# A delta-rule chunk scan: its triangular inverse in compact blocks of 32, and the head norms and turned outputs taken by groups

## The chip, the cores and the metric

The kernel runs on one core of one Trainium2 chip, as one program. The metric is device time in microseconds (us) for one execution, inputs in HBM to output in HBM. The kernel before took a median of 3159.22 us in 3 runs (3155.52 to 3159.49).

## The reference

Two models of two layers each are run one after the other on 256 tokens of width 1024. The change lies in the last mixer of the second model, a delta rule over 512 tokens (256 of context, 256 of the sequence), 16 heads of 64, in both directions, and in what follows it. (One small edit is at the kernel's very start.)

```python
def rwkv7_scan(r, w, k, v, kk, a, S):
    def step(S, inp):
        rt, wt, kt, vt, kkt, at = inp
        sa = jnp.einsum("bhvk,bhk->bhv", S, -kkt)
        S = S * wt[:, :, None, :] + sa[..., None] * (kkt * at)[:, :, None, :] + vt[..., None] * kt[:, :, None, :]
        return S, jnp.einsum("bhvk,bhk->bhv", S, rt)

def rwkv_out(y, p, kvec, lnx, w_o):
    y = head_layernorm(from_heads(y), lnx[0], lnx[1], RW_HEADS, r.dtype)   # mean and variance over each head's 64
    bonus = jnp.sum((r * k * kvec[2]).reshape(bn, L, RW_HEADS, RW_HEAD), axis=-1, keepdims=True) * v...
    return ((y + bonus.reshape(bn, L, D)) * g) @ w_o
```

## The kernel before

The kernel is written by hand, engine by engine: each engine has one program, and semaphores (`signal(...)`) join them. Each instruction of VectorE, ScalarE and GpSimd waits for the one before it on its engine (`Line.turn`, L72); TensorE's wait only where the code says so. Most of the kernel is matrix products in three passes (`x_high`, `x_low`, `w_high`, `ring_low`); these are not touched.

**The scan** is done in chunks of 64 tokens: 8 chunks forward, then 8 in the other direction, so 16 steps n, and one round more (n = 16) that finishes the last. The 16 heads stand as two groups g of 8; a group's 8 heads stand as four columns a by two halves i of the 128 partitions. Inside a chunk the delta rule is a lower triangular system, and the kernel inverts its matrix by products. The helper `quarters` does for each (a, i) one 64x64 by 64x64 product in fp32: eight products an operation (`one`), sixteen for two (`pair`). Each product in fp32 stands in the trace as two LDWEIGHTS and two MATMUL. The product for i = 0 uses rows and columns 0 to 63 of the array, that for i = 1 rows and columns 64 to 127.

One chunk of one group takes twelve steps, S0 to S11, and each `yield` in `scan_pe`, `scan_act`, `scan_dve` and `scan_pool` ends one:

- S0: `cum` (sums of the log decays) of chunk n and `w` of chunk n-1. S1: `us` of n-1. S2: `lta` of n (the two attention matrices), then `y` of n-1 (only where the chunk belongs to the sequence: n-1 = 4 to 7 and 12 to 15, called late) and `s` (the state) of n-1.
- S3: `n2`. S4: `n3`, `n4`. S5: `p`. S6: `f0`, `m2`. These invert the blocks of 8 on the diagonal.
- S7 to S11: `q2`, `m3`, `q3`, `m4`, `q4` join blocks of 8 to 16, 16 to 32 and 32 to 64; `mt`, `fab` and (late) `rab` lie between, as other operands of the chunk.

Between two steps the result goes from PSUM to SBUF through ScalarE (`n2`, `n4`, `f0`, `m2`, `m3`, `m4`, ...) or VectorE (`tft`, `n3`, `p`, `q2`, `q3`, `q4`, ...). GpSimd masks `lt` for `m2`, `m3`, `m4` (`mj1` to `mj3`). `lead` runs group 0 six steps ahead and then takes the groups in turn, a step of one, a step of the other, on every engine. So S6 of one group stands beside S0 of the other.

**After the scan** (`rwkv_pe`, `rwkv_act`, `rwkv_dve`): VectorE takes the layer norm of all heads in eight instructions over 2048 columns. Then for k = 0 to 7 TensorE turns the rows (`trs`), VectorE copies the halves out, scales, adds and gates them (five instructions a k), and only after k = 7 does TensorE start the output projection with the weights `rwo`, 32 products of 128x128 by 512 columns in fp32. The tiles `rwo` (0,1), (1,0), (1,1) are loaded once the norm's `on_ok` is given, since the scan uses ring slots as scratch.

**At the start** all engines wait for the constants and for the parameters `prm` before their first instruction, VectorE also for x.

Of the kernel before, what the change touches and what calls it, by code (L numbers as in the profile page):

```python
# [16 lines left out]
WS = 2048  # L17
# [173 lines left out]
def tile_plan(dr):  # L191
# [54 lines left out]
    plan.append((("rw2", 1), dr["rw2"], WS))  # L246
    plan.append((("rg2",), dr["rg2"], 1024))
    for n in range(2):
        for g in range(2):
            plan.append((("rwo", n, g), dr["rwo"][n, g], WS))  # L250
# [26 lines left out]
def program(nc, dr, out):  # L277
    ctx = ExitStack()
    with ctx:
# [224 lines left out]
        def norm_act(A, q):  # L504
# [7 lines left out]
            if q == FFN1[0]:  # L512
                split_act(A, ("gu", 0, 0))
            to = XT if q in RAW else xh(cols)
# [36 lines left out]
        def norm_dve(D, q):  # L551
# [3 lines left out]
            if q == FFN1[0]:  # L555
                split_dve(D, ("gu", 0, 0))
            for k in range(8):
# [1771 lines left out]
        joins = C("joins").rearrange("p (z m j) -> p z m j", z=2, m=3)  # L2329
        eye = C("eye")  # L2330
        hs = C("hs")
        PAIR = eye.unsqueeze(1).unsqueeze(1).to_broadcast([128, 2, 4, 64])
# [17 lines left out]
        STFT, SIT, SUT, SATB, SRAB, SKA, SRH = [[blocks(2) for _ in TWO] for _ in range(7)]  # L2350
        SE13 = [unit(2).rearrange("p (k t) -> p k t", k=4) for _ in TWO]
        SAL, SBE, SE2, SLT, SMJ, STD, SMT, SWW, SUS = [[blocks() for _ in TWO] for _ in range(9)]
# [43 lines left out]
        def act_names(n):  # L2396
            new, m = n < 16, n - 1
            return ([(n, "e13"), (n, "e2")] * new + [(m, "w"), (m, "us")] * (n > 0)
                    + [(n, x) for x in ("lta", "n2", "n4", "f0", "m2", "m3")] * new
                    + [(n, "fab")] * (new and feeds(n)) + [(n, "m4")] * new)  # L2400

        def dve_names(n):
            new, m = n < 16, n - 1
            return ([(n, "ak"), (n, "pc"), (n, "tft"), (n, "it")] * new + [(m, "y")] * (n > 0 and late(m))
                    + [(m, "s")] * (n > 0 and feeds(m)) + [(n, x) for x in ("n3", "p", "q2", "mt", "q3")] * new
                    + [(n, "rab")] * (new and late(n)) + [(n, "q4")] * new)
# [3 lines left out]
        def scan_keys(names):  # L2410
# [5 lines left out]
        sc_p = [signal(f"sc_p{g}", [(n, x) for n in range(16) for x in ("br", "mj1", "mj2", "mj3")]) for g in TWO]  # L2416
        on_ok, onr_ok, onn_ok = [signal(n, [0]) for n in ("on_ok", "onr_ok", "onn_ok")]
        yt2_mm, rg_mm, yg_ok = [signal(n, range(8)) for n in ("yt2_mm", "rg_mm", "yg_ok")]
        yc_ok = signal("yc_ok", range(8))
        wo_mm = signal("wo_mm", TWO)  # L2420
# [3 lines left out]
                  "fab": "fab", "m4": "m4"}  # L2424
# [9 lines left out]
        def double(g, key):  # L2434
            return scan_bank(g, key).rearrange("p (y k t) -> p y k t", y=2, k=4)

# [23 lines left out]
        def scan_pe(T, g):  # L2460
            te = T.eng
            al, be, lt, mj, td, mt, ww, us = [x[g] for x in (SAL, SBE, SLT, SMJ, STD, SMT, SWW, SUS)]
# [17 lines left out]
            def one(key, *terms):  # L2480
                take(key)
                quarters(single(g, key), terms, mm(key))

# [5 lines left out]
            for n in ROUNDS:  # L2489
# [25 lines left out]
                if old:  # L2515
                    te.wait_ge(*a_[m, "w"])
                    te.wait_ge(*d_[m, "q4"])
# [13 lines left out]
                yield  # L2531
                if new:
                    te.wait_ge(*d_[n, "tft"])
                    pair((n, "n2"), (tt_, tf), (tf, tt_))
                yield
                if new:
                    te.wait_ge(*d_[n, "it"])
                    te.wait_ge(*a_[n, "n2"])
                    one((n, "n3"), (itt, uu))
                    one((n, "n4"), (uu, tq))  # L2540
                yield
                if new:
                    te.wait_ge(*a_[n, "n4"])
                    te.wait_ge(*d_[n, "n3"])
                    one((n, "p"), (tq, SIT[g][:, 1]))
                yield
                if new:
                    te.wait_ge(*d_[n, "p"])
                    one((n, "f0"), (tf, eye))
                    te.wait_ge(*p_[n, "mj1"])  # L2550
                    one((n, "m2"), (mj, tf))
                yield
                for lev in (2, 3):
                    if new:
                        te.wait_ge(*a_[n, f"m{lev}"])
                        pair((n, f"q{lev}"), (uu, tt_), (tt_, uu))
# [6 lines left out]
                    if new:  # L2563
                        te.wait_ge(*d_[n, f"q{lev}"])
                        te.wait_ge(*p_[n, f"mj{lev}"])
                        one((n, f"m{lev + 1}"), (mj, tf))
                        if lev == 2 and feeds(n):
                            pair((n, "fab"), (al, eye), (be, eye))
                    yield
                if new:  # L2570
                    te.wait_ge(*a_[n, "m4"])
                    one((n, "q4"), (uu, tt_))
                yield

        def scan_act(A, g):
            se = A.eng
            e13, e2, lt, ww, us = [x[g] for x in (SE13, SE2, SLT, SWW, SUS)]
# [10 lines left out]

            for n in ROUNDS:
                new, old, m = n < 16, n > 0, n - 1  # L2590
                if n == 8 and g == 0:
# [15 lines left out]
                if new:  # L2607
                    se.wait_ge(*d_[n, "tft"])
                    if old:
                        se.wait_ge(*p_[m, "mj3"])  # L2610
                    A.copy(lt, double(g, (n, "lta"))[:, 0], a_((n, "lta")))
                yield
                if new:
                    take_both(SUT[g], (n, "n2"))
                yield
                if new:
                    take(tq, (n, "n4"))
                yield
                yield
                if new:  # L2620
                    take(STFT[g][:, 0], (n, "f0"))
                    take(uu, (n, "m2"), -1.0)
                yield
                yield
                if new:
                    take(uu, (n, "m3"), -1.0)
# [4 lines left out]
                if new:  # L2631
                    take(uu, (n, "m4"), -1.0)
                yield
                yield

        def scan_pool(G, g):
# [3 lines left out]
            for n in ROUNDS:  # L2640
# [13 lines left out]
                if new:  # L2654
                    ge.wait_ge(*a_[n, "lta"])
                    G.tt(SMJ[g], SLT[g], bm(joins[:, z, 0, :], 4), ALU.mult, p_((n, "mj1")))
# [4 lines left out]
                if new:  # L2661
                    ge.wait_ge(*mm[n, "m2"])
                    G.tt(SMJ[g], SLT[g], bm(joins[:, z, 1, :], 4), ALU.mult, p_((n, "mj2")))
                yield
                yield
                if new:
                    ge.wait_ge(*mm[n, "m3"])
                    G.tt(SMJ[g], SLT[g], bm(joins[:, z, 2, :], 4), ALU.mult, p_((n, "mj3")))
# [4 lines left out]
        def over(x):  # L2673

            return x.unsqueeze(2).to_broadcast([128, 2, 4, 64])

        def scan_dve(D, g):
# [6 lines left out]
            for n in ROUNDS:  # L2684
# [12 lines left out]
                if new:  # L2697
                    ve.wait_ge(*mm[n, "lta"])
                    D.tt(tft, double(g, (n, "lta")), over(near[:, z:z + 2, :]), ALU.mult, d_((n, "tft")))
# [16 lines left out]
                yield  # L2716
                yield
                if new:
                    ve.wait_ge(*mm[n, "n3"])
                    D.tt(it[:, 1], it[:, 1], single(g, (n, "n3")), ALU.add, d_((n, "n3")))  # L2720
                yield
                if new:
                    ve.wait_ge(*mm[n, "p"])
                    D.tt(tft[:, 1], it[:, 1], single(g, (n, "p")), ALU.add, d_((n, "p")))
                yield
                yield
                for lev in (2, 3):
                    if new:
                        ve.wait_ge(*mm[n, f"q{lev}"])
                        D.tt(tft, tft, double(g, (n, f"q{lev}")), ALU.add, d_((n, f"q{lev}")))  # L2730
# [9 lines left out]
                if new:  # L2740
                    ve.wait_ge(*mm[n, "q4"])
                    D.tt(STD[g], tft[:, 0], single(g, (n, "q4")), ALU.add, d_((n, "q4")))
# [45 lines left out]
        def rwkv_pe(T):  # L2788
# [47 lines left out]
            lead(scan_pe(T, 0), scan_pe(T, 1))  # L2836
            te.wait_ge(*onn_ok[0])
            te.wait_ge(*landed(("rg2",)))
            w = raw(("rg2",))
            for k in range(8):  # L2840
                T.bank(k % 4, yc_ok[k])
                trs(T, [(bank(k % 4)[0:64, 128 * c:128 * c + 128], YZ[:, c, k, :]) for c in FOUR], yt2_mm(k))
                T.bank(4 + k % 4, yg_ok[k])
                T.mm(bank(4 + k % 4)[:, 0:256], w[:, 128 * k:128 * k + 128], GS, True, True,
                     w_free(("rg2",)) if k == 7 else rg_mm(k))
            gate_pe(T, ("r", 0))
            te.wait_ge(*yg_ok[7])
            for n in TWO:
                for g in TWO:
                    key = ("rwo", n, g)  # L2850
                    te.wait_ge(*landed(key))
                    w = raw(key)
                    for tb in TWO:
                        b = 2 * n + tb
                        if g == 0:
                            T.bank(b, wo_d[n] if tb else wo_a[n])
# [536 lines left out]
```

## Time and profile before

| what | us |
|---|---|
| runs, median (lowest to highest) | 3159.22 (3155.52 to 3159.49) |
| profiled execution, its own time | 3160.5 |
| its span in the profile | 3158.7 |
| PE busy / DVE busy / ACT busy / POOL busy | 2906.1 / 1662.3 / 1217.0 / 117.7 |
| granted TensorE clock, mean | 0.953 of full |

PE is TensorE's matmuls, PEld its weight loads, DVE VectorE, ACT ScalarE, POOL GpSimd. All the matmuls of the kernel stand on L165 (a helper), so operations are told apart by tiles and shapes: the scan's are `64*64 64x64`, and run from 2368.7 to 2852.2 us of the span. A matmul's duration (219 ns for 64x64) is its way through the array; many overlap, so the cost of one is the distance between two starts.

### The profile page before, as it was taken

Reading aid. Unit: us, or ns where it says so; the run is one execution under the profiler, and the core shown is the slowest. Engines: PE = TensorE matmul, PEld = TensorE weight load, DVE = VectorE, ACT = ScalarE, POOL = GpSimd, SP = SyncE. Lnnn points to the kernel's source line nnn. Section 1 sums busy time; section 2 is a strip of 40 time slices with the busy share of each in tenths; the row PEclk is TensorE's granted clock in tenths of the full one; section 3 lists DMA queues with packets and bytes.
Section 4 is the critical chain, followed back from the end, with each engine's and each line's share of the span. In section 5 each row is a group of like instructions: output and inputs, shape, how many; then the busy total and the mean of one; then the engine's idle time right before and its main releaser. Section 6 shows DMA issues by size and latency. Waiting matters only on the chain.

```text
span 3158.7 us, 65576 instructions
## 1 busy us (share of the span) xinstructions
PE 2906.1 (92%) x28304; PEld 2435.2 (77%) x28304; DVE 1662.3 (53%) x2467; ACT 1217.0 (39%) x1839; POOL 117.7 (4%) x152
## 2 busy tenths in 40 slices
PE   8999999999999998997977999897999999996997
PEld 8977799898778987776656777673548989993886
DVE  5545655454655554214565777436424544555885
ACT  5445554443555443223433323233113334331333
POOL 0000000000000000000000000000002222220000
PEclk9999999999999999997888999998998999998999
DMA  6444344455443543430001343221200000002343
GB/s 241 180 167 174 122 165 177 174 180 186 165 169 112 184 150 140 173 141 28 2 23 54 147 156 137 100 73 51 94 33 4 4 4 17 4 4 107 133 148 107
DMA packets 49983, 349.87 MB, mean 111 GB/s; under 512 B 5792, under 2 KB 5792, under 8 KB 9248
## 3 DMA queue, kind: packets, MB, share of 16 engines
q1 hardware_dynamic: 49248, 343.56, 30.3%
q8 instruction: 225, 3.69, 0.5%
q0 software_dynamic: 448, 2.11, 0.2%
q14 instruction: 62, 0.51, 0.0%
HBM read 344.61 MB, written 1.05 MB: 109 GB/s over the span
## 4 chain that ended last, share of the span: by engine, by line
PE 78%; DVE 14%; ACT 5%; issue 2%; DMA 1%; DVEq 0%; ACTq 0%; SPq 0%
PE psum L165 78%; DVE arena L98 3%; DVE wide L87 2%; DVE ring_low L87 2%; DVE arena L87 2%; ACT w_high L144 1%; DMA ring<-in_evt 1%; PE psum L170 1%; ACT arena L140 1%; ACT wide L138 1%; ACT wide L144 0%; ACT L138 0%; ACT ring L144 0%; DVE wide L98 0%; DVE h L98 0%
## 5 line engine op out<-in xcount | busy, mean ns | idle before, releaser
L87 DVE TENSOR_TENSOR ring_low<-ring,w_high 128x2048 fp32r<-128x2048 f32 (+3 forms) x254 | 560.3, 2206 | 578.8 <-ACT w_high L144 574.1
L144 ACT ACTIVATE w_high<-ring 128x2048 fp32r<-128x2048 f32 (+3 forms) x254 | 468.9, 1846 | 823.5 <-PE psum L165 480.9
L165 PE MATMUL psum<-x_high,w_high 128*128 128x256 f32 (+1 forms) x2040 | 633.6, 311 | 12.8 <-DVE x_low L87 6.4
L165 PE MATMUL psum<-x_high,ring_low 128*128 128x256 f32 (+1 forms) x2040 | 626.6, 307 | 0.0
L165 PE MATMUL psum<-x_low,w_high 128*128 128x256 f32 (+1 forms) x2040 | 626.5, 307 | 0.0
L165 PE MATMUL psum<-wide,ring 64*64 64x64 f32 (+3 forms) x4400 | 413.5, 267 | 23.2 <-DVE wide L87 12.8
L165 PEld LDWEIGHTS psum<-x_high,w_high 128*128 128x128 f32 x2040 | 390.0, 191 | 49.7 <-issue 15.9
L165 PEld LDWEIGHTS psum<-x_high,ring_low 128*128 128x128 f32 x2040 | 390.0, 191 | 18.6
L165 PEld LDWEIGHTS psum<-x_low,w_high 128*128 128x128 f32 x2040 | 390.3, 191 | 17.2
L165 PEld LDWEIGHTS psum<-wide,ring 64*64 64x64 f32 (+2 forms) x4400 | 293.5, 146 | 121.1 <-issue 89.4
L165 PE MATMUL psum<-w_high,x_high 128*128 128x512 f32 (+2 forms) x720 | 281.2, 391 | 15.9 <-issue 14.0
L165 PE MATMUL psum<-ring_low,x_high 128*128 128x512 f32 (+2 forms) x720 | 276.7, 384 | 0.0
L165 PE MATMUL psum<-w_high,x_low 128*128 128x512 f32 (+2 forms) x720 | 276.6, 384 | 0.0
L165 PE MATMUL psum<-wide 64*64 64x64 f32 (+3 forms) x6832 | 242.7, 219 | 9.6 <-ACT wide L144 4.8
L165 PEld LDWEIGHTS psum<-wide 64*64 64x64 f32 (+2 forms) x6832 | 215.7, 133 | 25.1 <-ACT wide L144 9.3
L144 ACT ACTIVATE wide<-psum 128x256 f32<-128x256 f32 (+3 forms) x255 | 114.7, 450 | 238.7 <-PE psum L165 229.1
L98 DVE SCALAR_TENSOR_TENSOR arena<-arena,prm 128x256 f32<-128x256 f32 x396 | 192.1, 485 | 14.1
L165 PEld LDWEIGHTS psum<-w_high,x_high 128*128 128x128 f32 x720 | 139.8, 194 | 52.9 <-issue 24.4
L87 DVE TENSOR_TENSOR wide<-wide,psum 128x512 f32<-128x512 f32 (+1 forms) x164 | 91.5, 558 | 168.7 <-PE psum L165 162.5
L165 PE MATMUL psum<-w_high,h_high 128*128 128x512 f32 x440 | 171.9, 391 | 4.1 <-DVE ring_low L87 4.1
L165 PE MATMUL psum<-ring_low,h_high 128*128 128x512 f32 x440 | 171.2, 389 | 0.0
L165 PE MATMUL psum<-w_high,h_low 128*128 128x512 f32 x440 | 171.2, 389 | 0.0
(191 smaller groups left out, 3450.4 us busy)
## 6 DMA issues: line engine op xcount, KB each, us to landing
ring<-in_f_gu SPq DMA_DIRECT2D x88, 1024.0 KB, 4.8
ring<-in_w_mod SPq DMA_DIRECT2D x48, 1024.0 KB, 5.0
ring<-in_fu SPq DMA_DIRECT2D x44, 1024.0 KB, 4.9
ring<-in_f_dn SPq DMA_DIRECT2D x40, 1024.0 KB, 4.8
ring<-in_w_in SPq DMA_DIRECT2D x28, 1024.0 KB, 4.8
ring<-in_fd SPq DMA_DIRECT2D x20, 1024.0 KB, 4.9
ring<-in_rkvr SPq DMA_DIRECT2D x12, 1024.0 KB, 4.8
ring<-in_w_out SPq DMA_DIRECT2D x8, 1024.0 KB, 4.8
```

The source lines that it names most:

```text
L87: self.done(self.eng.tensor_tensor(o, a, b, op), then)
L98: self.done(self.eng.scalar_tensor_tensor(out=o, in0=a, scalar=s, in1=b, op0=op0, op1=op1), then)
L138: self.done(self.eng.activation(o, i, f, bias=bias, scale=scale), then)
L140: self.done(self.eng.activation(o, i, f, bias=bias, scale=scale, accum_out=total), then)
L144: self.done(self.eng.activation(o, i, ACT.Copy, scale=scale), then)
L165: ins = self.eng.matmul(o, l, r, start=a, stop=z)
L170: ins = self.eng.transpose(o, i, ident[0:i.shape[0], 0:i.shape[0]])
```

## The change

- **Inverse in 32s.** The operands of the inverse (`tft`, `it`, `SUT`, `lt`, `mj`) hold only the two 32x32 blocks on the diagonal of each 64x64 matrix, stacked on the partitions: 128 partitions by 4 columns by 32. `sixteenths` does for each a four products of 32x32 by 32x32, on the four squares of 32 on the array's diagonal: sixteen products an operation. The copies and additions out of PSUM shrink to half their columns. `attention32` makes `lta` in the same compact form. The last join, 32 to 64, is done by `across` (`m4`, `q4`): eight products of 32x32, on two squares at a time. `q4` goes out by ScalarE now, in two instructions of 32 partitions, as do `m4` and a third part of `lta`; VectorE spreads the blocks (`td`, one instruction of 256 columns). `mj3` is gone from GpSimd.
- **Norms by groups.** The head sums and sums of squares are taken per chunk and group inside the scan's last rounds (n = 13 to 16, four instructions of 256 columns at S3), the root and the factors per group. `turned_pe` turns by products with `eye` straight into the layout wanted, and VectorE takes two instructions a k. Group 0's outputs and `rwo` (0,0) are put into the rounds in which group 1 ends.
- **Loads and waits.** `rwo` (0,0) is loaded ahead of `rg2`; the other three tiles wait for the last `y` of both groups instead of `on_ok`. The first instructions wait for the constants (VectorE also for x) only; `prm` is waited for where its values are used first.

```diff
+            def sixteenths(o, l, r, then=None):
+                for a in FOUR:
+                    for q in FOUR:
+                        p = slice(32 * q, 32 * q + 32)
+                        T.mm(o[p, a, :], l[p, a, :], r[p, a, :] if len(r.shape) == 3 else r[p, :], True, True,
+                             then if a == 3 and q == 3 else None)
+            def across(key, rows, to, l, r):
+                take(key)
+                o = narrow_single(g, key)
+                for a in FOUR:
+                    for i in TWO:
+                        p = rows32(i, rows)
+                        T.mm(o[rows32(i, to), a, :], l[p, a, :], r[p, a, :], True, True, mm(key) if a == 3 and i else None)
...
-                    pair((n, "lta"), (al, ka), (ka, al))
+                    attention32((n, "lta"), z, al, ka)
...
-                    pair((n, "n2"), (tt_, tf), (tf, tt_))
+                    pair32((n, "n2"), (tt_, tf), (tf, tt_))
...
+        def outputs_pe(T, g):
+            yield from scan_pe(T, g)
+            for k in range(4 * g, 4 * g + 4):
+                turned_pe(T, k)
+                yield
+            if g == 0:
+                rows_out_pe(T, 0, 0)
...
+        def outputs_dve(D, g):
+            yield from scan_dve(D, g)
+            for k in range(4 * g, 4 * g + 4):
+                y = KK[:, k, 0:256]
+                D.eng.wait_ge(*yt2_mm[k])
+                D.stt(y, bank(4 * g + k % 2)[:, 0:256], lx[:, 0, k:k + 1], BV[:, k, :], ALU.mult, ALU.add, yc_ok(k))
+                D.eng.wait_ge(*(w_free[("rg2",)] if k == 7 else rg_mm[k]))
+                D.tt(y, y, bank(4 * g + 2 + k % 2)[:, 0:256], ALU.mult, yg_ok(k))
                 yield
...
+                if m >= 12:
+                    c = chunk(m) - 4
+                    y, s, a = YZ[:, c, hs, :], ntmp[:, :].rearrange("p (k v) -> p k v", k=4), NM[:, c, hs]
+                    D.red(a, y, ALU.add)
+                    D.stt(y, bc(a, 64), -1.0 / 64, y, ALU.mult, ALU.add)
+                    D.tt(s, y, y, ALU.mult)
+                    D.red(NV[:, c, hs], s, ALU.add)
...
-            for s in (ld_cst, ld_prm):
-                eng.wait_ge(s, 16)
+            eng.wait_ge(ld_cst, 16)
```

TensorE, one steady half round of the scan (from one group's `cum`, 64x128, to the other's), before; `wide`, `ring` and `cx` are the memories in which the operands lie, and one row is so many products of one shape:

```order
L165 MATMUL psum<-cx,wide 64x128 x8
L165 MATMUL psum<-wide,ring 64x64 x8
L165 MATMUL psum<-cx,wide 64x64 x8
L165 MATMUL psum<-wide,ring 64x64 x8
L165 MATMUL psum<-ring 64x64 x8
L165 MATMUL psum<-wide 64x64 x16
L165 MATMUL psum<-wide,ring 64x64 x16
L165 MATMUL psum<-ring,wide 64x64 x8
```

The same place now:

```order
L165 MATMUL psum<-cx,wide 64x128 x8
L165 MATMUL psum<-wide,ring 64x64 x8
L165 MATMUL psum<-cx,wide 32x32 x16
L165 MATMUL psum<-wide 32x32 x16
L165 MATMUL psum<-ring 64x64 x8
L165 MATMUL psum<-wide 32x32 x32
L165 MATMUL psum<-wide,ring 64x64 x8
L165 MATMUL psum<-wide,ring 32x32 x16
L165 MATMUL psum<-ring,wide 32x32 x16
L165 MATMUL psum<-wide,ring 32x32 x8
```

The order of the operations is kept; those of the inverse have twice the products, each a quarter of the work of a 64x64, and products of 32 and of 64 now alternate.

VectorE after the last `y` of the scan, before:

```order
L106 TENSOR_REDUCE small<-wide 128x32
L92 TENSOR_SCALAR small<-small 128x32
L87 TENSOR_TENSOR wide<-wide,small 128x2048
L87 TENSOR_TENSOR wide<-wide 128x2048
L106 TENSOR_REDUCE small<-wide 128x32
L94 TENSOR_SCALAR small<-small 128x32
L115 RECIPROCAL small<-small 128x32
L87 TENSOR_TENSOR wide<-wide,small 128x2048
L102 COPY wide<-psum 64x256 x2
L94 TENSOR_SCALAR wide<-wide,prm 128x256
L87 TENSOR_TENSOR wide<-wide 128x256
L87 TENSOR_TENSOR wide<-wide,psum 128x256
```

Now, at group 1's end:

```order
L106 TENSOR_REDUCE small<-wide 128x4
L98 SCALAR_TENSOR_TENSOR wide<-small,wide 128x256
L87 TENSOR_TENSOR ntmp<-wide 128x256
L106 TENSOR_REDUCE small<-ntmp 128x4
L94 TENSOR_SCALAR small<-small 128x4x4
L115 RECIPROCAL small<-small 128x4x4
L98 SCALAR_TENSOR_TENSOR wide<-psum,prm,wide 128x256
L87 TENSOR_TENSOR wide<-wide,psum 128x256
L98 SCALAR_TENSOR_TENSOR wide<-psum,prm,wide 128x256
L87 TENSOR_TENSOR wide<-wide,psum 128x256
L87 TENSOR_TENSOR wide<-wide,small 128x256 x4
```

Only the last chunk's sums of one group are left behind the last `y`; the pairs with `psum,prm,wide` are group 0's outputs, which stand between group 1's norm instructions.

## Rows read from the trace of the kernel before

**Rows 1.** The chain that ended last, share of the span by engine.
```profile
PE 78%; DVE 14%; ACT 5%; issue 2%; DMA 1%; DVEq 0%; ACTq 0%; SPq 0%
```

**Rows 2.** Busy time by stretch: an early and a late round, norm, turned outputs, projection.
```profile
core 0: us, PE busy (x) PEld busy (x) DVE busy (x) ACT busy (x) POOL busy (x), PEclk, DMA share, GB/s
2690.50:2717.00 26.50, 25.46 (x804) 24.67 (x801) 13.73 (x27) 10.50 (x24) 6.43 (x8) 1.00 0.01 4
2775.40:2806.50 31.10, 30.24 (x969) 29.44 (x968) 16.15 (x31) 10.50 (x24) 8.06 (x10) 1.00 0.02 4
2852.20:2865.40 13.20, 0.03 (x1) 0.04 (x2) 12.57 (x9) 0.23 (x1) 0.00 (x0) 0.64 0.11 31
2865.40:2885.70 20.30, 14.27 (x65) 10.60 (x65) 16.75 (x40) 0.06 (x1) 0.00 (x0) 0.67 0.48 186
2885.70:2915.60 29.90, 29.84 (x64) 12.81 (x64) 6.68 (x6) 7.33 (x11) 0.00 (x0) 0.93 0.30 106
```

**Rows 3.** TensorE's instructions in order of time, in the scan: start, us, count.
```profile
2672.25 2.99 PE L165 MATMUL psum<-wide 64*64 64x64 f32 x96
...
2368.74 1.09 PE L165 MATMUL psum<-cx,wide 64*64 64x128 f32 x16 [1.07 <-DVE wide L87]
```

**Rows 4.** The same, an earlier stage, around products on 64 rows by 32 columns.
```profile
1484.62 1.05 PE L165 MATMUL psum<-cst,wide 128*128 128x128 f32 x8
1485.60 0.76 PE L165 MATMUL psum<-wide 64*32 64x32 f32 x64
1486.29 0.48 PE L165 MATMUL psum<-arena 128*128 128x256 f32 x1
```

**Rows 5.** The same, products of 32x32 by 128 columns on the four diagonal squares.
```profile
1569.45 1.95 PE L165 MATMUL psum<-arena,wide 32*32 32x128 f32 x64
```

**Rows 6.** Groups by shape in the early round: count, busy us, mean ns, idle before.
```profile
L144 ACT ACTIVATE wide<-psum 128x256 f32<-128x256 f32 x10 | 3.8, 384 | 4.7 <-PE psum L165 4.3
L87 DVE TENSOR_TENSOR wide<-wide,psum 128x512 f32<-128x512 f32 x4 | 2.8, 688 | 6.1 <-PE psum L165 6.0
...
L144 ACT ACTIVATE wide<-psum 128x512 f32<-128x512 f32 x4 | 2.4, 598 | 3.1 <-PE psum L165 3.1
...
L87 DVE TENSOR_TENSOR wide<-wide,psum 128x256 f32<-128x256 f32 x4 | 1.7, 422 | 2.5 <-PE psum L165 2.4
```

**Rows 7.** VectorE in order of time behind the scan.
```profile
2852.64 2.29 DVE L106 TENSOR_REDUCE small<-wide 128x32 f32<-128x2048 f32 x1
...
2866.47 0.87 DVE L102 COPY wide<-psum 64x256 f32<-64x256 f32 x2 [1.16 <-PE psum L170]
2867.37 0.41 DVE L94 TENSOR_SCALAR wide<-wide,prm 128x256 f32<-128x256 f32 x1
```

**Rows 8.** Stretches of the scan's start (group 0 alone, then both) and end.
```profile
2371.20:2374.60 3.40, 1.97 (x32) 1.78 (x32) 1.46 (x4) 0.00 (x0) 0.72 (x1) 0.50 0.00 0
...
2384.80:2388.20 3.40, 3.40 (x59) 3.27 (x57) 0.77 (x2) 0.98 (x2) 0.73 (x1) 0.50 0.02 5
2388.20:2391.60 3.40, 3.12 (x102) 2.98 (x102) 2.18 (x5) 0.98 (x2) 0.78 (x1) 0.99 0.00 0
...
2849.00:2852.20 3.20, 2.29 (x64) 2.02 (x64) 0.01 (x1) 1.98 (x3) 0.00 (x0) 1.00 0.02 5
```

**Rows 9.** DMA issues of the page: KB, us to landing.
```profile
h<-in_x SPq DMA_DIRECT2D x1, 1024.0 KB, 6.7
...
cst<-in_cst SPq DMA_DIRECT2D x1, 896.0 KB, 4.6
...
prm<-in_prm SPq DMA_DIRECT2D x1, 418.0 KB, 7.3
```

**Rows 10.** The kernel's first instructions in order of time (SyncE's queue, ScalarE).
```profile
1.18 0.42 SPq L3140 DMA_DIRECT2D h<-in_x  x1
...
9.05 1.28 ACT L138 ACT_TABLE_LOAD   x1 [9.05 <-DMA prm<-in_prm]
...
10.64 0.63 ACT L140 ACTIVATE arena<-h 128x512 f32<-128x512 f32 x1
```

More of the change, by code:

```diff
@@ L2399, in act_names @@
                     + [(n, x) for x in ("lta", "n2", "n4", "f0", "m2", "m3")] * new
-                    + [(n, "fab")] * (new and feeds(n)) + [(n, "m4")] * new)
+                    + [(n, "fab")] * (new and feeds(n)) + [(n, "m4"), (n, "q4")] * new)
         def dve_names(n):
@@ L2564, in scan_pe @@
                         te.wait_ge(*d_[n, f"q{lev}"])
[L2565 to L2568, printed above, removed]
+                        if lev == 3:
+                            te.wait_ge(*a_[n, "lta"])
+                            across((n, "m4"), z, 1 - z, mj4, tf)
+                        else:
+                            te.wait_ge(*p_[n, "mj2"])
+                            one32((n, "m3"), mj, tf)
+                            if feeds(n):
+                                pair((n, "fab"), (al, eye), (be, eye))
                     yield
@@ L2576, in scan_act @@
             se = A.eng
[L2577 removed]
+            e13, e2, td, ww, us = [x[g] for x in (SE13, SE2, STD, SWW, SUS)]
+            lt, mj4, u4 = SLM[g][:, 0], SJU[g][:, 0], SJU[g][:, 1]
             uu, tq = SUT[g][:, 0], SUT[g][:, 1]
@@ L2609, in scan_act @@
                     if old:
-                        se.wait_ge(*p_[m, "mj3"])
-                    A.copy(lt, double(g, (n, "lta"))[:, 0], a_((n, "lta")))
+                        se.wait_ge(*p_[m, "mj2"])
+                    p4 = scan_bank(g, (n, "lta"))[:, 0:384].rearrange("p (y k t) -> p y k t", y=3, k=4)
+                    A.copy(lt, p4[:, 0])
+                    take_half(mj4, p4[:, 2], z, (n, "lta"))
+                if n == 16 and g == 0:
+                    A.act(small[:, 216:217], ident[:, 0:1], ACT.Sqrt)
+                yield
+                if n == 16:
+                    yield
+                    yield
+                    se.wait_ge(*on_ok[g])
+                    A.act(NR[:, :, 4 * g:4 * g + 4], NR[:, :, 4 * g:4 * g + 4], ACT.Sqrt, onr_ok(g))
+                    yield
+                    yield
+                    yield
+                    return
+                if new:
+                    se.wait_ge(*mm[n, "n2"])
+                    A.copy(SUT[g], narrow_double(g, (n, "n2")), a_((n, "n2")))
                 yield
                 if new:
[L2614 to L2617, printed above, removed]
+                    take32(tq, (n, "n4"))
                 yield
@@ L2698, in scan_dve @@
                     ve.wait_ge(*mm[n, "lta"])
-                    D.tt(tft, double(g, (n, "lta")), over(near[:, z:z + 2, :]), ALU.mult, d_((n, "tft")))
+                    D.tt(tft, narrow_double(g, (n, "lta")), over(near[:, z:z + 2, :]), ALU.mult, d_((n, "tft")))
                     D.tt(it, PAIR, tft, ALU.subtract, d_((n, "it")))
```

257 lines of the change are left out of this document (156 added, 101 removed).

## The prediction, made before the changed kernel ran

> **What bounds the kernel now.** I read first the chain that ended last [rows 1]: TensorE holds 78% of it, so a stage in which TensorE is busy gets shorter by what is taken from its instruction stream. Then the stretches of the stage [rows 2]. An early round of the scan takes 26.5 us and TensorE is busy for 25.5, a late one 31.1 and 30.2; VectorE, ScalarE and GpSimd are about half, 40% and a quarter busy. Behind the scan it is another picture: 13.2 us with TensorE idle (norm), 20.3 us in which VectorE is busy for 16.75 (turned outputs), 29.9 us of projection with TensorE full. So the inverse must be priced on TensorE, and the norms and outputs by what of VectorE's work goes behind other work.
>
> **What a product costs there.** 96 MATMUL of 64x64 span 2.99 us [rows 3]; less the 0.22 of the last, 2.77 / 95 = 29.2 ns from start to start, two for each fp32 product. For `cum`, (1.09 - 0.27) / 15 = 54.6 ns. Check: an early round has 800 MATMUL, 32 of `cum` and 768 others: 32 x 0.0546 + 768 x 0.0292 = 24.2 us. The round takes 26.5, so 2.3 us are waits that the two groups do not cover for each other.
>
> **What a product of 32x32 costs.** None is in the trace, so two rows bound it. The 64 of 32x32 by 128 columns, on the same four squares and into one bank, span 1.95 us: (1.95 - 0.27) / 63 = 26.7 ns each [rows 5], half the 54.6 of `cum`, which has two squares at once and the same 128 columns. So four squares do run at once, and by columns alone a 32-column product would cost about a quarter of that, 7 ns. The other limit is the stream itself: 64 MATMUL on 64 rows by 32 columns span 0.76 us [rows 4], (0.76 - 0.19) / 63 = 9.0 ns, with the 32 columns that the new ones have. I take 9.0, the row nearest in size, just behind a change of shape as here. Ends: 7 and 10.8 (the whole 0.69 us until the next operation, over 64). `across` has only two squares at a time: twice a square's time. A square's time is bounded above by four times 9.0 = 36 and below by 29.2 (a 64's start to start over two squares is 58.4, half the columns); I take 32, so 16 ns each.
>
> The Trainium skill (TensorE: Matmul & The Clock Gate, Part 1) says that two matmuls never start less than about 25 ns apart, however small. Here 64 of them started 9.0 ns apart [rows 4], so the trace disagrees; it remains a rival below.
>
> **The inverse, part by part, for one group and round.** Before: `n2`, `q2`, `q3`, `lta` 32 MATMUL each, `n3`, `n4`, `p`, `f0`, `m2`, `m3`, `m4`, `q4` 16 each, 256 x 29.2 = 7.48 us. After, in MATMUL: `n2`, `q2`, `q3` 64 each and `n3`, `n4`, `p`, `f0`, `m2`, `m3` 32 each are 384 x 9.0 = 3.46; `lta` 64 x 9.0 + 16 x 16 = 0.83; `m4`, `q4` 32 x 16 = 0.51. Sum 4.80, less by 2.68; two groups, 5.36 us a round.
>
> Added: the shape of the products now changes about 18 times a round (between S0's 64s and the other group's 32s, around `mt`, `fab`, `lta`, and back). Around a change the trace has [rows 4]: eight of 128x128 start (1.05 - 0.275) / 7 = 0.11 us apart, which puts the next start at 1484.62 + 8 x 0.11 = 1485.50; it came at 1485.60. So 0.09 us a change, 1.6 us a round. Bounds: 0, if changes among small shapes are free or stand in a wait, and 0.2, twice the one seen. This agrees with the skill (TensorEngine Tiling (Array Packing), Key Properties), by which a change of tiling mode drains the engine; it gives no price.
>
> Waits stay at 2.3. For them: ScalarE's copies go from 256 to 128 columns, (598 - 384) / 2 = 0.11 us less, VectorE's additions from 512 to 256, 0.27 less [rows 6]. Against them: less work of the other group covers them. Followed step by step: S9 and S3 leave about 0.2 before `m4` and 0.25 before `n3` (ScalarE's 0.38 and 0.3 of way, the array's 0.22 and the hand-over, against 0.25 of `m4` in between); `m4` and `q4` leave through two ScalarE instructions each, 0.28 x 2 + 0.3 = 0.86 us, of which 0.15 are bare; `p` waits 0.15 to 0.3 for `n3`. That is 0.8 a half round, 1.6 a round, and ScalarE's order (`e13`, `e2`, `w` ahead of the other group's `f0`, `m2`) adds 0.3 to 0.7. `mj3` costs nothing: GpSimd is a quarter busy.
>
> A round: 26.5 - 5.36 + 1.6 = 22.7, 3.8 us less; 16 rounds, 61 us. In the late rounds of the second direction the head sums (four instructions of 0.42, each group, on VectorE between two steps) show in part: 1 us in each of four, -4. **Scan: 57 us.** Ends: no price for changes and 8.35 ns, 85; 0.2 a change, 28; 10.8 ns, 35.
>
> **Behind the scan.** Before, from the last product (2852.2) to the end of the projection (2915.6): 63.4 us [rows 2]. After, from group 1's last `y`, on TensorE: group 0's turned outputs k = 1 to 3 and `rwo` (0,0) come first. A turned k has 16 MATMUL of 29.2 and two of 256 columns, each half of the projection's 29.84 / 64 = 0.47 [rows 2], plus two changes: 1.1 us, x3 = 3.3. `rwo` (0,0): a quarter of 29.9, 7.5. By 10.8 us group 1's norm is long done: six small instructions (about 2.1), a root (0.5), four of 0.42: 4.5 instead of 13.2 [rows 2, 7]. Then four k, 4.4 (VectorE has two instructions of 0.42 for each, 0.9, instead of 2.4 with the half-wide copies [rows 7]); `rwo` (0,1) 7.5; the gate's turns, 16 MATMUL, 1.8, hidden before, bare now; the rest 14.9. Sum 39.4: **24 us less**. The three tiles load while `rwo` (0,0) runs. Ends 18 (a group's outputs stay bound by VectorE, 2 us, and the loads come late by 4) and 27 (the clock falls for less long than in the 33 us of rows 2 at 0.64 and 0.67).
>
> **The start.** ScalarE's first instruction waits for `prm` until 9.05 [rows 10], x lands at 1.18 + 6.7 = 7.9 [rows 9, 10], and the table load of 1.28 can go ahead once the constants are in (about 5.4). The squares begin at 7.9 instead of 10.64: 2.7 less, of which I take 2.5; ends 0 (the first weights not there earlier) and 2.7.
>
> **Sum.** 57 + 24 + 2.5 = 83.5 from the profiled execution's own 3160.5 (span 3158.7) is 3077; that execution is 1.3 over the median shown, so 3076.
>
> **The rivals.**
> A. *The waits grow.* What TensorE gives back is waited for: each group is a chain of twelve steps, and with 9.4 instead of 12.1 us of TensorE work a group and round less is covered; or changes cost 0.2. For it: at the scan's end, where one group is alone, TensorE is busy for only 2.29 of 3.2 us [rows 8]. Against: the other group fills most. At 4.7 us of waits a round, 38 us go: 3114.
> B. *The clock falls, and it is slower.* TensorE would be near 80% busy with smaller products. For it: at the scan's start it ran at 0.50 of full while 58% busy, and came back to full after a stretch that was full at the lower clock [rows 8]. Against: at the scan's end it was 72% busy at 1.00 [rows 8], and at the low clock the work doubles, which fills the engine and ends it. A round wholly at 1.2 GHz costs 2 x 18.8 + 1.6 = 39 instead of 22.7, so 16 more; it decides from 5 rounds of 16. At 8: 3076 + 130 = 3206.
> C. *Starts have a floor of 25 ns.* By the mechanism of this kernel: 992 MATMUL of 32 a round at 25 ns are 24.8, with 9.2 of others, 1.6 and 1 of waits 36.6, +10.1 a round, 161 less 26.5: 3294. The 9.0 ns of rows 4 speak against it. (It is the skill's figure named above.)
> D. *It doesn't do what it says:* only two squares at a time with 32 columns, 16 ns each: about +1.7 a round, 27, and the rest gains 26.5: 3160, no change. Rows 5 speak against it.
>
> **How the numbers follow.** Forecast 66% (own range 3054 to 3094, from the ends of the price of a start and of a change), A 21%, B 8%, C 2%, D 3%. The range 3052 to 3120 holds the forecast's case and most of A. A difference of 0.2% (6 us) is what a measurement of this kernel can tell. Faster: forecast and A, 87%, and a part of B below five rounds, 1%: 88%. Same: D, 3%. Slower: the rest of B, and C, 9%.
>
> **What would show it.** Early rounds of about 22.7 us and late of 27 from `cum` to `cum`; 32x32 MATMUL about 9 ns apart, in rows such as x64 in under 0.8 us; gaps of 0.1 at a change of shape; PEclk at 1.00 through the scan; some 40 us from the last `y` to the projection's end with no TensorE gap over 2 us; ScalarE's first squares near 8 us. Wrong would be starts of 15 ns or more, rounds over 25 with the waits in front of `n3`, `p`, `q4`, or a clock at 0.50 inside the scan.

## The result, and the profile after

| | median us | lowest to highest | runs |
|---|---|---|---|
| before | 3157.8 | 3155.52 to 3159.49 | 4 |
| after | 3343.54 | 3341.55 to 3346.77 | 4 |

The ratio is 1.059, 95% interval 1.0571 to 1.0608: 186 us slower. Forecast was 3076 (3052 to 3120), which is 82 faster. The profiled execution of after took 3341.55, with a span of 3339.7.

First the page of after: instructions and busy time of each engine, the row of instruction transfers, and the chain that ended last.

```profile
span 3339.7 us, 81263 instructions
## 1 busy us (share of the span) xinstructions
PE 2975.6 (89%) x36080; PEld 2466.3 (74%) x36080; DVE 1610.8 (48%) x2487; ACT 1232.0 (37%) x2001; POOL 70.7 (2%) x120
...
q8 instruction: 286, 4.69, 0.6%
...
PE 78%; DVE 11%; issue 6%; ACT 3%; DMA 1%; DVEq 0%; ACTq 0%; SPq 0%
```

Against [rows 1], VectorE lost 3 points of the chain, as meant, and "issue", time in which an engine waits for nothing that the profile shows, went from 2% to 6%. The kernel has 15,687 instructions more (before has 65,576), nearly all of them TensorE's: 7,776 MATMUL and as many LDWEIGHTS (weight loads). In q8, a queue that brings instructions, 225 packets became 286. By number they are TensorE's, and 256 make a packet: 286 x 256 = 73,216, against 72,160 MATMUL and LDWEIGHTS on the page and some waits that it doesn't count; before, 225 x 256 = 57,600 against 56,608.

Then the stretches, as in [rows 2]: the whole scan from its first `cum` to the last `y`, what is behind it, an early round and a late one.

```profile
core 0: us, PE busy (x) PEld busy (x) DVE busy (x) ACT busy (x) POOL busy (x), PEclk, DMA share, GB/s
...
2365.40:3054.90 689.50, 536.02 (x21490) 474.20 (x21492) 200.81 (x479) 190.40 (x554) 68.13 (x112) 0.76 0.02 7
3054.90:3094.50 39.60, 38.49 (x214) 19.65 (x208) 17.22 (x30) 7.60 (x12) 0.00 (x0) 1.00 0.48 186
2467.70:2506.60 38.90, 29.30 (x1285) 26.79 (x1280) 10.89 (x27) 11.39 (x35) 3.50 (x6) 0.76 0.02 4
2970.60:3015.50 44.90, 34.54 (x1450) 31.57 (x1442) 16.38 (x38) 11.46 (x35) 5.01 (x8) 0.80 0.02 4
```

The balance by its parts, each against before:

- the scan starts at 2365.4, before at 2368.7: -3.3
- the scan takes 689.5, before 483.5: +206
- behind it 39.6, before 63.4: -23.8
- the rest of the span (to 3339.7) 245.2, before 243.1: +2.1

Sum +181, which is the difference of the two profiled executions (3341.55 - 3160.5). So the whole loss stands in the scan. An early round takes 38.9 us there instead of 26.7, a late one 44.9 instead of 31.2.

TensorE in order of time inside one early round (start, us, operation, count; in brackets the idle time before and what ended it):

```profile
2478.24 0.28 PE L165 MATMUL psum<-ring,wide 64*64 64x64 f32 x3
2478.45 0.45 PE L165 MATMUL psum<-wide 32*32 32x32 f32 x32
2478.83 1.15 PE L165 MATMUL psum<-cx,ring 64*64 64x64 f32 x32
2479.91 0.50 PE L165 MATMUL psum<-wide 32*32 32x32 f32 x35
2481.19 1.45 PE L165 MATMUL psum<-wide 32*32 32x32 f32 x127 [0.79 <-issue]
2484.96 2.26 PE L165 MATMUL psum<-wide 32*32 32x32 f32 x92 [2.32 <-issue]
```

The 32 MATMUL of 32x32 in the second row start (0.45 - 0.19) / 31 = 8.4 ns apart, if 0.19 is taken for the way of the last one. This is the price that was forecast. But then the engine stops twice, and what ends both stops is "issue", no other engine. Between the two stops stand 127 MATMUL with their 127 weight loads, that is 254 instructions, some 256 with the waits that are not shown, as many as one packet of q8 (4.69 MB / 286 = 16.4 KB) holds. The bursts of experiment 2 show the same number with nothing else going on.

The transfers of that round, in 40 slices of 0.97 us:

```profile
GB/s 0 0 0 17 0 0 0 17 0 0 0 17 0 0 0 17 0 0 0 17 0 0 0 17 8 0 0 17 0 0 0 17 0 0 0 17 0 0 0 17
...
q8 instruction: 10, 0.16, 1.6%
```

Every fourth slice holds one packet of q8 (the 8 is a packet of another queue), one every 3.9 us, so 256 / 3.9 = 66 instructions a us. The round's LDWEIGHTS and MATMUL are 2565 / 38.9 = 65.9 a us. And before? The same view of the kernel before, over 40 us of its scan (slices of 1 us):

```profile
GB/s 0 16 0 0 0 16 0 0 0 16 0 0 0 16 0 0 8 0 16 0 0 0 16 0 0 16 0 0 0 16 0 0 0 0 16 0 0 0 0 16
```

Nearly the same beat: an early round had (810 + 808) / 26.7 = 60.6 instructions a us. The kernel before ran at some 90% of what the supply delivers, and hardly waited for it: in its whole scan TensorE's idle time that "issue" ended is 3.2 us in 10 times, and in this early round there is none.

### The profile page after: what moved, and what is told of

It reads as the page before. It is cut to its first block, busy times and chain, and to the rows that moved or that the text cites. A ratio compares the mean times of both kernels' runs of the same rounds, so it can differ in the third digit from the quotient of the medians.

```text
span 3339.7 us, 81263 instructions
## 1 busy us (share of the span) xinstructions
PE 2975.6 (89%) x36080; PEld 2466.3 (74%) x36080; DVE 1610.8 (48%) x2487; ACT 1232.0 (37%) x2001; POOL 70.7 (2%) x120
## 3 DMA queue, kind: packets, MB, share of 16 engines
q1 hardware_dynamic: 49248, 343.56, 29.2%
q8 instruction: 286, 4.69, 0.6%
## 4 chain that ended last, share of the span: by engine, by line
PE 78%; DVE 11%; issue 6%; ACT 3%; DMA 1%; DVEq 0%; ACTq 0%; SPq 0%
PE psum L165 78%; DVE arena L98 3%; DVE ring_low L87 2%; DVE arena L87 2%; ACT w_high L144 1%; DVE wide L87 1%; ACT arena L140 1%; PE psum L170 1%; DMA ring<-in_evt 1%; ACT arena L144 0%; DVE wide L98 0%; DVE h L98 0%; DVE x_low L87 0%; ACT L138 0%; ACT wide L144 0%
## 5 line engine op out<-in xcount | busy, mean ns | idle before, releaser
L165 PE MATMUL psum<-wide,ring 64*32 64x32 f32 (+4 forms) x3888 | 395.3, 281 | 26.6 <-issue 13.2
L165 PEld LDWEIGHTS psum<-wide,ring 64*32 64x32 f32 (+3 forms) x3888 | 273.8, 152 | 127.8 <-issue 103.9
L165 PE MATMUL psum<-wide 32*32 32x32 f32 (+2 forms) x14000 | 266.3, 211 | 110.3 <-issue 103.8
L165 PEld LDWEIGHTS psum<-wide 32*32 32x32 f32 (+2 forms) x14000 | 218.7, 123 | 145.4 <-issue 120.5
L144 ACT ACTIVATE wide<-psum 128x128 f32<-128x128 f32 (+5 forms) x383 | 125.0, 326 | 406.8 <-PE psum L165 320.2
L87 DVE TENSOR_TENSOR wide<-wide,psum 128x256 f32<-128x256 f32 (+2 forms) x164 | 65.8, 402 | 320.3 <-PE psum L165 316.3
L165 PE MATMUL psum<-ring,wide 64*64 64x64 f32 (+3 forms) x2528 | 178.4, 245 | 16.6 <-issue 16.4
```

Source lines behind the costliest of these rows:

```text
L87: self.done(self.eng.tensor_tensor(o, a, b, op), then)
L144: self.done(self.eng.activation(o, i, ACT.Copy, scale=scale), then)
L165: ins = self.eng.matmul(o, l, r, start=a, stop=z)
```

## The experiments

Three theories. **F**: TensorE's instructions arrive at no more than about 66 a us, whatever they do, and a round of after is 2588 of them (2565 LDWEIGHTS and MATMUL, and the waits). **B**: the granted clock fell (0.76 in the round above), rival B of the prediction. **H**: the changes of shape and the hand-overs between engines are waited for, rival A. Experiments 2 to 5 ran once each; nine runs of the kernel before in the job of 1 to 4 lie between 3153.48 and 3160.52, and the differences below are far larger.

### 1. All but the inverse

The kernel before with the norms and outputs by groups, the loads and the first waits of the change, and its own inverse in 64s (no `sixteenths`, `attention32`, `across` or compact operands):

```diff
+            for k in range(4 * g, 4 * g + 4):
+                turned_pe(T, k)
+                yield
+            if g == 0:
+                rows_out_pe(T, 0, 0)
...
                     pair((n, "n2"), (tt_, tf), (tf, tt_))
```

> The kernel before with the changed kernel's norms and outputs by groups, its start and its loads, and the inverse left in products of 64x64. Theory F (TensorE's instructions are fetched 256 at a time, about 3.85 us a fetch, 66.5 a microsecond; the 32s doubled the instructions of the inverse and the scan is bound by that): the scan keeps its rounds of 26.5 and 31.1 us, since its instructions stay, and the rest gains what the changed kernel's trace shows outside the scan, 2.6 at the start and about 18 to 24 behind the scan: 3131 to 3137, ratio about 0.992. Rival B (the slow part is the clock, which falls whenever TensorE has short gaps) expects the same here unless the group-wise end brings the clock down in the late rounds: then 3150 or more. Rival G (the norm instructions put into the rounds n = 13 to 16 cost much of the loss): the last rounds grow from 31.1 to over 35 and the total is above 3158.

Measured: 3137.93 (3135.55 to 3139.39, 5 runs) against 3157.09 for before in the same job (3153.48 to 3160.52, 9 runs); ratio 0.9936, 95% interval 0.9922 to 0.9949. It beats both kernels, the one before by only 0.6%, which is clear of the noise; F had 3131 to 3137. Its stretches:

```profile
2364.80:2850.70 485.90, 461.20 (x13812) 437.90 (x13814) 253.47 (x479) 175.11 (x394) 115.31 (x144) 0.98 0.03 7
2850.70:2890.30 39.60, 38.45 (x212) 19.61 (x208) 17.22 (x30) 7.61 (x12) 0.00 (x0) 1.00 0.49 186
```

The scan takes 485.9 again (2.4 more than before: the head sums and the first of the turned outputs are in it), and behind it are the same 39.6 us as in after. A late round takes 31.2 us, as before, so the norm instructions in the last rounds (G) aren't the loss. So the whole loss comes with the inverse in 32s: after takes 206 us more than this kernel.

### 2. Four bursts of products that nobody waits for

```diff
+            for j in range(1200):
+                p = slice(32 * (j % 4), 32 * (j % 4) + 32)
+                T.mm(bank(2)[p, 0:32], ident[p, 0:32], ident[p, 32:64], True, True)
+            for j in range(64):
+                T.mm(bank(2), ident, h[:, j % 2, 0:512], True, True)
+            for j in range(1200):
+                p = slice(64 * (j % 2), 64 * (j % 2) + 64)
+                T.mm(bank(2)[p, 0:64], ident[p, 0:64], ident[p, 64:128], True, True)
...
```

They stand ahead of the scan in the kernel before, and the fourth repeats the second; the whole took 3411.5, of which only the bursts are of interest.

> The kernel before with four bursts of unused products on TensorE right ahead of the scan: 1200 products of 32x32x32 in fp32 (2400 pairs of weight load and matmul, 4800 instructions) that go round the four diagonal squares, 64 of 128x128 by 512 columns, 1200 of 64x64x64 on two squares, 64 of 128x128 by 512. Nothing waits inside a burst. F: the first burst starts at 8 to 9 ns a pair while instructions are in store, and then goes on at 256 instructions per 3.85 us, 30 ns a pair, with gaps: 35 to 60 us in all, with the instruction DMA at its highest rate; the clock may fall in it. Without F, squares and columns alone: 2400 x 9 = 22 us, without gaps. C (a floor of 25 ns between starts): 60 us, but evenly spaced from the first pair on. D (two squares only): 16 ns a pair, 38 us, evenly spaced. The burst of 64x64 takes 2400 x 29.2 = 70 us under all of them, since 68.5 instructions a microsecond is just about F's limit.

The first seven rows of TensorE in the burst of 32s:

```profile
2370.67 2.10 PE L165 MATMUL psum<-cst 32*32 32x32 f32 x226 [1.07 <-DVE wide L87]
2374.72 1.29 PE L165 MATMUL psum<-cst 32*32 32x32 f32 x128 [1.95 <-issue]
2378.74 1.93 PE L165 MATMUL psum<-cst 32*32 32x32 f32 x128 [2.73 <-issue]
2382.49 1.93 PE L165 MATMUL psum<-cst 32*32 32x32 f32 x128 [1.82 <-issue]
2386.23 1.93 PE L165 MATMUL psum<-cst 32*32 32x32 f32 x128 [1.81 <-issue]
2389.98 1.93 PE L165 MATMUL psum<-cst 32*32 32x32 f32 x128 [1.81 <-issue]
2393.72 1.93 PE L165 MATMUL psum<-cst 32*32 32x32 f32 x128 [1.81 <-issue]
```

The transfers from 2376 to 2396 us, in 40 slices of 0.5 us:

```profile
GB/s 0 0 0 0 0 0 0 33 0 0 0 0 0 0 0 33 0 0 0 0 0 0 33 0 0 0 0 0 0 0 33 0 0 0 0 0 0 33 0 0
q8 instruction: 5, 0.08, 2.1%
```

The burst of 64s, as TensorE's rows show it:

```profile
2492.43 70.22 PE L165 MATMUL psum<-cst 64*64 64x64 f32 x2400
```

And two stretches of the windows, the first inside the burst of 32s, the second that of 64s:

```profile
2382.49:2393.72 11.23, 5.79 (x384) 5.39 (x384) 0.00 (x0) 0.00 (x0) 0.00 (x0) 0.50 0.02 4
2492.40:2562.60 70.20, 70.20 (x2402) 70.10 (x2401) 0.00 (x0) 0.00 (x0) 0.00 (x0) 1.00 0.02 4
```

This is the clearest picture of the mechanism. No other engine is at work and nothing is waited for, yet 128 MATMUL and 128 weight loads run, and then the engine stands still until the next 256 are there. From start to start it is 3.74 to 3.75 us in the last four rows, 68.4 instructions a us; over all blocks from the third row on it is 3.47 to 4.02 and 3.71 in the mean, 69.0 a us. The first 226 ran (2.10 - 0.19) / 225 = 8.5 ns apart, out of what was in store. That speaks against both rivals of even spacing, 25 ns and 16 ns. The burst took 65.6 us in all; I had given the store more than the some 450 instructions it held, hence the miss of the 35 to 60 expected.

The packets' own records place them in this beat. Each starts 1.1 to 1.7 us behind the start of a block of 128 pairs and is on its way for 0.9 to 1.5 us; the next block starts 1.2 to 1.5 us behind its end. So there is one packet at a time, and a block that starts late follows a packet that came late.

The 64s ran without one stop at 29.2 ns a MATMUL, which is 68.4 instructions a us as well. Whether the array or the supply set this pace isn't told apart; a product of 64x64 takes about the time in which the supply brings one. The clock was 0.50 in the block rows of the 32s and 1.00 in the 64s, and the packets came 3.72 us apart in the one and 3.69 in the other, in the mean. H has no part in it, and no difference of the rate with the clock shows.

### 3. More instructions into the kernel before

```diff
+                    for j in range(120):
+                        q = j % 4
+                        p = slice(32 * q, 32 * q + 32)
+                        T.mm(spill[p, 256:288], tf[p, 0, 0:32], eye[p, 0:32], True, True)
```

> The kernel before with 120 unused products of 32x32x32 put ahead of f0 in each chunk of each group, into the free half of its bank: 960 instructions more a round, which brings the count to that of the changed kernel (some 2580 early, 2920 late), while the inverse is still done in 64s and only two changes of shape a group and round are added. F: rounds of 38.8 and 43.9 us as in the changed kernel, total 3158 + 16 x 12.5 = 3350 to 3360. By array and stream time: 480 pairs x 9 ns + 0.4 = 4.7 us a round, 31 and 36, total 3233. Rival H (the loss comes from the many changes of shape or from the longer chain of waits through two-piece copies, neither of which is here) also expects 3233.

Measured 3380.33. F was near (20 to 30 us under), the sum without F 147 short. The added MATMUL are 480 a round, 480 x 8.5 ns = 4.1 us of TensorE's time; the round grew by 13.3. An early round:

```profile
2477.20:2517.20 40.00, 34.96 (x1290) 33.68 (x1286) 13.49 (x27) 10.50 (x24) 6.50 (x8) 0.87 0.02 4
```

2576 / 40.0 = 64.4 a us. The kernel before gets slower than after by products that leave its inverse in 64s and its hand-overs as they are, and bring the number of instructions to about that of after.

### 4. Half the instructions in the inverse

After, with each two products of 32x32 by 32 columns in `sixteenths` issued as one by 64 columns. The weights of two of the four columns a are left out, so those results are not the reference's; operations, copies and waits are the same.

```diff
-                for a in FOUR:
+                for a in (0, 2):
...
-                        T.mm(o[p, a, :], l[p, a, :], r[p, a, :] if len(r.shape) == 3 else r[p, :], True, True,
+                        T.mm(o[p, a:a + 2, :], l[p, a, :],
+                             r[p, a:a + 2, :] if len(r.shape) == 3 else r[p, :].unsqueeze(1).to_broadcast([32, 2, 32]),
```

> The changed kernel with sixteenths doing two of the four columns with one weight load (eight products of 32x32 by 64 columns instead of sixteen by 32; the weights of the second and fourth column are left out, so the inverse is another one). The columns streamed, the changes of shape and the copies stay; the instructions fall by 768 a round. F: early rounds (2588 - 768) / 66.5 = 27.4, late ones 32.3 us, total about 3342 - 16 x 11.1 = 3160. B, if the clock were the cause by itself: streamed work is about the same, so it goes on toggling and rounds stay above 35: over 3280. H (changes of shape, chain of waits): rounds stay near 38, 3330 or more.

Measured 3156.87, 187 less than after, at F's 3160 and far from H's and B's. The same columns go through the same squares, with the same hand-overs. (It also halves the number of MATMUL, so a price for each MATMUL isn't excluded here but by the burst.) An early round:

```profile
2442.50:2471.10 28.60, 23.76 (x900) 20.97 (x896) 11.10 (x27) 11.53 (x35) 3.52 (x6) 0.93 0.02 5
```

1796 / 28.6 = 62.8 a us: even with half of the sixteen products of each operation gone the round stands close to the supply's limit (4.3 us of it are idle time that "issue" ended), and is no shorter than before's.

### 5. The same columns as in 3 in an eighth of the instructions; half the dose of 3

```diff
-                    for j in range(120):
+                    for j in range(15):
...
-                        T.mm(spill[p, 256:288], tf[p, 0, 0:32], eye[p, 0:32], True, True)
+                        T.mm(spill[p, 256:512], tf[p, 0, 0:32], tf[p, :, :].rearrange("p k t -> p (k t)"), True, True)
```

> The kernel before with 15 unused products of 32x32 by 256 columns ahead of f0 in each chunk and group: the same 3840 columns as the 120 products of 32x32x32 of e3_more_instructions (which took 3380), in an eighth of the instructions. F (TensorE's instructions come in at no more than 66.5 a us): an early round has 1623 + 120 = 1743 instructions, 26.2 us, which is no limit beside 26.5; what is left is the array's own time, 60 MATMUL x 26.7 ns = 1.6 us and about 0.5 for changes of shape, so rounds of 28 to 29 and 3158 + 16 x 2.1 = 3192. Rival S (it is the columns, the squares or the changes of shape of the added products that cost): as e3, rounds of 38 to 40 and 3380.

```diff
-                    for j in range(120):
+                    for j in range(60):
```

> The kernel before with 60 unused products of 32x32x32 ahead of f0 in each chunk and group, half of e3_more_instructions. F: an early round has 1623 + 480 = 2103 TensorE instructions, over 66.5 a us 31.6 us; a late one 1958 + 480 = 2438, 36.7; 16 rounds of +5.3 give 3158 + 85 = 3243. Rival S (array's time alone): 240 MATMUL x 9 ns = 2.2 us and 0.4 for changes of shape, early rounds of 29.1, 3158 + 42 = 3200. Rival B (the cost comes from the granted clock falling, all or nothing): either as S, or a jump to near e3's 3380.

Measured: 3214.72 with 15 wide products, 3256.99 with 60 small ones (the kernel before took 3155.38 in the same job). An early round with the wide ones:

```profile
2470.00:2500.30 30.30, 29.45 (x868) 26.68 (x866) 13.85 (x26) 10.51 (x25) 7.22 (x9) 1.00 0.02 4
```

An early round with the 60 small ones:

```profile
2447.40:2479.60 32.20, 28.60 (x1043) 27.37 (x1043) 13.44 (x26) 10.18 (x24) 6.42 (x8) 1.00 0.02 4
```

The wide ones cost 3.6 us a round where the same columns in small products cost 13. This is 23 us more than expected, by an error of mine: [rows 5] are of 128 columns, and 256 take twice their 26.7 ns. The round shows 30 of them in 1.92 us, (1.92 - 0.27) / 29 = 57 ns each; 60 x 57 ns = 3.4 us. So S, by which the columns, squares or changes of shape cost, falls.

The half dose gives 2086 / 32.2 = 64.8 instructions a us, at a clock of 1.00 in this round, and TensorE stops four times, 4.7 us in all, each time ended by "issue". This takes B away as the cause: a round can be bound by the supply without any fall of the clock. It took 14 us more than F's sum: early rounds took 32.2 us for 31.6, late ones 37.8 for 36.7, with only (1202 + 1199) / 37.8 = 63.5 a us.

All early rounds side by side, MATMUL and LDWEIGHTS in each:

| kernel | instructions | round us | a us | clock | idle, ended by "issue", us |
|---|---|---|---|---|---|
| before | 1618 | 26.7 | 60.6 | 1.00 | 0 |
| 15 wide products added | 1734 | 30.3 | 57.2 | 1.00 | 0 |
| half the inverse's products | 1796 | 28.6 | 62.8 | 0.93 | 4.3 |
| 60 small added | 2086 | 32.2 | 64.8 | 1.00 | 4.7 |
| after | 2565 | 38.9 | 65.9 | 0.76 | 9.4 |
| 120 small added | 2576 | 40.0 | 64.4 | 0.87 | 4.4 |

From 2086 instructions upward the round's length goes with their number, at 64.4 to 65.9 a us, and not with the clock. How much of a round is idle doesn't go with the number alone: at a lower clock TensorE is also busy for longer.

## Why the prediction was wrong, point by point

**What bounds the kernel.** The sentence that "a stage in which TensorE is busy gets shorter by what is taken from its instruction stream" was then worked out with the array's time in place of the stream's. The stream became longer, not shorter: 1618 to 2565 instructions a round.

**What a product of 32x32 costs: the step that failed.** "I take 9.0, the row nearest in size." The price itself holds, as 8.4 ns in after's row x32 and 8.5 ns in the first 226 of the burst. But [rows 4] are 64 MATMUL alone in a stage of large products, 128 instructions out of the store. For the 992 small MATMUL a round the price is that of two instructions at 65.9 a us, 30.3 ns for a MATMUL with its load, and in such a round that holds for the 64s too. The term by which a group's inverse falls from 7.48 to 4.80 us, less by 2.68, should have been made from numbers of instructions: 947 more a round, at 65.9 a us. The round that was forecast at 22.7 us took 2565 / 65.9 = 38.9; over the scan this turns -57 into +206. That the kernel before stood at 60.6 a us, and that its instruction packets came every 4 us, could be read before.

**Changes of shape.** The next 32x32 in after's rows starts at 2478.45, 0.15 us behind the last start of the 64s before it (2478.30), or 0.12 more than their pitch. Forecast 0.09. The size is about right at this place, and in a round that the supply binds it costs nothing of its own.

**The waits** (rival A) didn't grow: what TensorE waits for in the round is "issue". All the waits of the round that ended so:

```profile
PE psum L165 <- issue: 9.4, 8, 2.3
```

This is 9.4 us in 8 times, the longest 2.3, and no other engine is in that list. Over the whole scan "issue" ended 141.2 us of TensorE's idle time (3.2 before), all the other engines together 10.0 (20.8 before).

**The clock** (rival B) did fall, to 0.76 of full in the mean of the round, and of the clock alone B was right. But it isn't what made the round long: at 1.00 the half dose ran at 64.8 a us, at 0.76 after ran at 65.9, so the lower clock cost no time that the supply hadn't taken already. That it fell because TensorE stood idle for 9.6 of 38.9 us is likely, and not tested by itself.

**A floor of 25 ns between starts** (rival C) came out nearest in time, 3294, with a mechanism that is wrong: starts are 8.4 ns apart where there is a store. What the runs show is a mean of 29.0 ns (burst) to 30.3 ns (scan) for a MATMUL with its load, over 256 instructions at a time. So 3294 came near partly by luck: it charged 25 ns for each small MATMUL and nothing more for the 64s. Still, 2% was too little for a rival that said so nearly what a long stream does; the short row of 64 could speak against a floor, not against a limit of the supply.

**Two squares at a time** (rival D) is false: it had 16 ns from start to start, and 8.4 were measured.

**Behind the scan**: forecast 39.4 us, measured 39.6, in after and in experiment 1. The last group's norm is short and hidden, as said, and no load was late: TensorE stops once there, 1.0 us, ahead of `rwo` (0,0). VectorE in experiment 1, from the last sums on (start, us, operation, count):

```profile
2852.48 0.42 DVE L106 TENSOR_REDUCE small<-wide 128x4 f32<-128x256 f32 x1
...
2854.51 0.25 DVE L115 RECIPROCAL small<-small 128x16 f32<-128x16 f32 x1
...
2857.10 1.80 DVE L87 TENSOR_TENSOR wide<-wide,small 128x256 f32<-128x256 f32 x4
2863.22 0.48 DVE L98 SCALAR_TENSOR_TENSOR wide<-psum,prm,wide 128x256 f32<-128x256 f32 x1 [4.32 <-PE psum L165]
```

Against 13.2 us of norm in [rows 2, 7], the last group's rows are normed at 2858.9, while TensorE has `rwo` (0,0) until 2862.6; then VectorE waits for TensorE, no longer the other way.

**The start**: forecast 2.5. ScalarE's first square, [rows 10], now in after:

```profile
8.04 0.63 ACT L140 ACTIVATE arena<-h 128x512 f32<-128x512 f32 x1 [2.38 <-DMA h<-in_x]
```

It is 2.6 earlier, and so is TensorE's first product, 12.30 instead of 14.90; the scan starts 3.3 earlier. With what is behind the scan 26.5 us were forecast for this half of the change, and experiment 1 measured 19.2 by the medians. Its profiled execution is 21.6 shorter in span than before's: the scan starts 3.9 earlier and takes 2.4 more, behind it 23.8 are gained, and from the projection's end to the end of the span it is 246.8 instead of 243.1, which no run explains.

**The head sums** were to cost 4 us in the late rounds. In experiment 1 a late round with them takes 31.2 us, as before, with VectorE busy for 19.5 instead of 16.1, so they are hidden behind TensorE; the whole scan there is 2.4 longer.

**A rule that I passed over.** The Trainium skill (Runtime: NRT & Kernel Launch, Instruction fetch mechanics) says that an engine's instruction memory is refilled in blocks of 256 instructions by a DMA queue of its own. The trace agrees: 128 pairs between two stops, and 16.4 KB packets on q8. It also says that crossing a block costs little and is mostly hidden. Here that holds for the kernel before, and not for a stream of small products: 1.5 to 2.1 us of standing still in every 3.5 to 4.0 of the burst. The page has no rate; with it read beside the 225 packets, the limit would at least have been a rival. By the figure that it gives for TensorE's memory, 2048 instructions, the burst should have begun with far more than the 226 pairs that ran; what was in the store then no row shows.

What stays open: why the packets come no closer. One is on its way for about 1 us by its record, and its queue has a share of 1.6% of the transfer engines; no two of them start less than 3.29 us apart anywhere in before or in after. The beat of the burst, with a packet some 1.1 us behind each block's start and a block some 1.4 us behind each packet's end, looks as if one were fetched only when another is used up; what fills these two stretches no run shows. Nor was a round of 22.7 us with the supply out of the way ever seen: that the array would do it is not shown.

## What to carry to other kernels

Before cutting TensorE's work into smaller pieces, count its instructions per microsecond, weight loads and both passes of fp32 included, and look at the beat of the instruction queue's packets: here the ceiling was 64 to 69 a us, and a stage at 60 had no room for smaller products. A row that shows a short burst prices the array, not a long stream; take the price of a stream from one that is longer than the store (here some 450 instructions). And where a change has independent parts, time them apart: here 19 us of gain were under 206 of loss.

## What the runs showed of the hardware

- TensorE's instructions came in packets of 16.4 KB, and 256 ran between two stops; in a burst with nothing else going on one such block ran every 3.71 us in the mean (3.47 to 4.02), 69.0 instructions a us, at a clock of 0.50, and products of 64x64 at 1.00 ran at 68.4.
- In that burst a block started 1.2 to 1.5 us behind the end of a packet, and a packet 1.1 to 1.7 us behind the start of a block.
- In rounds of the scan bound by the supply the rate was 63.5 to 65.9, a little under the burst's.
- What was in store at the burst's start were some 450 instructions.
- MATMUL of 32x32 by 32 columns on four squares started 8.4 ns apart at a clock of 1.00, and by 256 columns 57 ns apart.
